# Mixing product tile by tile with two extra weight slots, the norm's factor moved into Exp and Gelu, and expert numbers found in two halves

## The reference, cut to what matters

```python
xn = rmsnorm_2(h, norm1_g)
q_a, k_a, v_a, q_b, k_b, v_b, gate_a, gate_b = split(xn @ w_in)
y_a = merge(moba_attention(...)) @ w_out_moba
y_b = merge(stick_breaking_attention(...)) @ w_out_sb
mixed = sigmoid(gate_a) * y_a + sigmoid(gate_b) * y_b
h = h + mixed @ w_mix_out
h = h + peer_ffn(rmsnorm_2(h, norm2_g), w_q, sub_keys, expert_u, expert_v)
return rmsnorm_2(h, final_norm_g)
```

```python
qh = (x @ w_q).reshape(8, 2, 128)
scores = einsum('hpc,hpnc->hpn', qh, sub_keys)            # 2 x 128 scores
s_top, i_top = top_k(scores, 16)                           # of each half
cand = s_top[0][:, None] + s_top[1][None, :]               # 256 sums
c_s, c_pos = top_k(cand, 16)                               # 16 experts of 16384
e = i_top[0][c_pos // 16] * 128 + i_top[1][c_pos % 16]
a = gelu(u[e] @ x); out += (softmax(c_s) * a) @ v[e]
```

## Time and profile before

| | |
|---|---|
| median of 3 runs | 1776.45 us (1774.53 to 1779.31) |
| profiled execution | 1774.82 us, span 1773.1 us |
| mean granted clock of TensorE | 0.981 of 2.4 GHz |
| busy: TensorE, VectorE, ScalarE, POOL | 1621.1, 1128.0, 849.2, 351.9 us |
| moved: gathers, other loads | 268.45 MB, 194.29 MB |

### The profile page before, as it was taken

How to read it: one execution, slowest core, us unless ns; L and a number is a source line. 1 busy time by engine, 2 the same in 40 slices (tenths; PEclk the granted TensorE clock), 3 DMA queues, 4 the chain that set the end, 5 groups by cost and what they waited for, 6 DMA issues and landing times.

```text
span 1773.1 us, 22582 instructions
## 1 busy us (share of the span) xinstructions
PE 1621.1 (91%) x8800; PEld 1222.6 (69%) x8800; DVE 1128.0 (64%) x1993; ACT 849.2 (48%) x1578; POOL 351.9 (20%) x368
## 2 busy tenths in 40 slices
PE   6999999999999999999989998899978788778786
PEld 5998998999898999899979997555522222222232
DVE  4747766555665776655555566778667667767744
ACT  4546635444455653544445644455444444444443
POOL 0100000000010000000040100555544444334440
PEclk9999999999999999999999999899999999999999
DMA  6544353555544346455544354999999999999996
GB/s 251 196 144 143 140 216 144 200 186 188 194 153 140 136 167 217 158 203 185 185 153 148 143 194 187 387 412 421 420 422 421 421 421 422 422 421 422 421 421 257
DMA packets 67066, 464.51 MB, mean 262 GB/s; under 512 B 7440, under 2 KB 9616, under 8 KB 11536
## 3 DMA queue, kind: packets, MB, share of 16 engines
q0 software_dynamic: 36864, 268.45, 36.5%
q1 hardware_dynamic: 29808, 194.29, 30.4%
q10 hardware_dynamic: 288, 0.33, 0.1%
HBM read 462.00 MB, written 1.05 MB: 261 GB/s over the span
## 4 chain that ended last, share of the span: by engine, by line
PE 67%; DMA 20%; DVE 5%; issue 4%; ACT 3%; POOL 0%; SPq 0%; POOLq 0%; ACTq 0%; DVEq 0%
PE acc L541 15%; PE acc L542 15%; PE acc L543 15%; DMA arena<-in_peer_uv,arena 8%; DMA row_w_lo<-in_peer_uv,arena 7%; PE acc L1621 4%; DMA row_w_hi<-in_peer_uv,arena 4%; PE acc L1624 4%; PE att L543 3%; PE att L542 3%; PE att L541 3%; DVE w_lo L537 1%; ACT w_hi L530 1%; PE att L839 1%; ACT gate_raw L1750 1%
## 5 line engine op out<-in xcount | busy, mean ns | idle before, releaser
L537 DVE TENSOR_TENSOR w_lo<-arena,w_hi 128x2048 fp32r<-128x2048 f32 x176 | 404.7, 2302 | 200.9 <-ACT w_hi L530 200.6
L530 ACT CAST w_hi<-arena 128x2048 fp32r<-128x2048 f32 x176 | 335.4, 1907 | 150.4 <-PE acc L543 139.0
L541 PE MATMUL acc<-xa_hi,w_hi 128*128 128x256 f32 x928 | 266.3, 287 | 0.0
L542 PE MATMUL acc<-xa_hi,w_lo 128*128 128x256 f32 x928 | 263.2, 284 | 0.0
L543 PE MATMUL acc<-xa_lo,w_hi 128*128 128x256 f32 x928 | 263.2, 284 | 0.0
L1742 ACT ACTIVATE arena<-arena 128x1 f32<-128x1 f32 x256 | 51.9, 203 | 313.8 <-DVE arena L2023 143.3
L2023 DVE SCALAR_TENSOR_TENSOR arena<-arena 128x1024 f32<-128x1024 f32 x114 | 139.4, 1223 | 84.7 <-DMA arena<-in_peer_uv,arena 84.6
L541 PEld LDWEIGHTS acc<-xa_hi,w_hi 128*128 128x128 f32 x928 | 178.5, 192 | 4.1 <-issue 3.1
L542 PEld LDWEIGHTS acc<-xa_hi,w_lo 128*128 128x128 f32 x928 | 178.5, 192 | 0.2
L543 PEld LDWEIGHTS acc<-xa_lo,w_hi 128*128 128x128 f32 x928 | 178.5, 192 | 0.0
L1621 PE MATMUL acc<-arena,gate_raw 128*128 128x512 f32 x228 | 129.5, 651 | 49.4 <-ACT gate_raw L1750 49.3
(11 more groups left out here) (295 smaller groups left out, 3352.4 us busy)
## 6 DMA issues: line engine op xcount, KB each, us to landing
arena<-in_units SPq DMA_DIRECT2D x176, 1024.0 KB, 4.8
arena<-in_bias SPq DMA_DIRECT2D x1, 2048.0 KB, 9.2
arena<-in_peer_uv,arena POOLq DMA_INDIRECT x114, 36.2
x_res<-in_x SPq DMA_DIRECT2D x2, 512.0 KB, 4.2
arena<-in_norm_mix_g SPq DMA_DIRECT2D x2, 512.0 KB, 6.6
arena<-in_norm_mlp_g SPq DMA_DIRECT2D x2, 512.0 KB, 6.5
arena<-in_norm_g SPq DMA_DIRECT2D x2, 512.0 KB, 5.7
arena<-in_final_norm_g SPq DMA_DIRECT2D x2, 512.0 KB, 5.7
```

What stands on the lines that cost most here:

```text
L530: nc.scalar.copy(w_hi[:, s, :], raw[HOME[g]]).then_inc(S["hi_ready"], 1)
L537: nc.vector.tensor_tensor(w_lo[:, s, :], raw[HOME[g]], w_hi[:, s, :].bitcast(F32), ALU.subtract).then_inc(S["lo_ready"], 1)
L541: nc.tensor.matmul(out_, lh, rh, start=first, stop=False)
L542: nc.tensor.matmul(out_, ll, rh, start=False, stop=False)
```

## The change

It has four parts.

1. The units of the mix come in the order 0, 2, 1, 3, and TensorE makes all four on tile 0 before it finishes tile 1. Mix 0 and pq 0 get weight slots of their own (`more_hi`, `more_lo`, laid over the biases, `mo` and `qk`); from yab 1 on the splits run three units ahead (`splits_at`). The loads of pq 5 and 6 wait for mix 0, since they lie where its parts are. The sub-keys are loaded ahead of unit ga2 0 and transposed after yab 0. Tile 1's queries of head 0 come after the whole mix.
2. The norm ahead of the experts no longer multiplies by one over the root: `hn` is x times the norm's weights, made half by half behind each add; the order of scores isn't changed by a positive factor for each token, and the factor is given as `scale` to Exp (of the score differences) and to Gelu. The squares (`peer_square`) come later, into memory of their own.
3. Head 0's first eight experts of tile 0 are looked up as soon as the eight largest sums are found, the next eight after; POOL waits for each eight. Tile 1's adds come behind head 0's whole routing on VectorE (`mix_second_tile`).
4. 18 places instead of 17, with other memory and other opening times: places 0 and 1 over mix 3's slot, 2 and 3 over `xa`, 4 and 5 over pq 0's slot, 6 and 7 over the raw slots of pq 2 and 3 (from items 6 and 8 on).

```diff
-PLACES = 17
-OPEN_FROM = [0] * 5 + [5, 6, 20, 30, 40, 50] + [72] * 6
+PLACES = 18
+OPEN_FROM = [0] * 4 + [4, 4, 6, 8, 20, 30, 40, 50] + [72] * 6
...
-    u += [("mix", i, "T") for i in range(4)] + [("pq", i, "F") for i in range(8)]
+    u += [("mix", i, "T") for i in (0, 2, 1, 3)] + [("pq", i, "F") for i in range(8)]
...
-SLOT = [g % RING for g in range(QUERY0 + 2)] + [(QUERY0 + h % 2) % RING for h in range(2, P_HEADS)]
+MIX0 = QUERY0 - 4
+SLOT = [g % RING for g in range(MIX0)] + [RING] + [(g - 1) % RING for g in range(MIX0 + 1, QUERY0)] + [RING + 1]
+SLOT += [SLOT[QUERY0 - 3 + (h + 1) % 2] for h in range(1, P_HEADS)]
...
-        rows_ring = slot_rows(q2) + [area("mo", 0, ROW), row_over("xa_hi", 0), row_over("xa_lo", 0)]
+        rows_ring = slot_rows(q3) + [row_over("xa_hi", 0), row_over("xa_lo", 0), area("mo", 0, ROW), area("qk", 0, ROW)]
...
+                if unit == ("ga2", 0, "F"):
+                    sp.wait_ge(S["hn_ready"], at("hn_ready", ("n1", TT - 1)))
+                    for h in range(HP):
+                        sp.dma_start(raw_keys[:, h, :], A["peer_sub_keys_2"][0, h // 2, h % 2]).then_inc(
+                            S["keys_loaded"], mark("keys_loaded", h, 16))
+                elif unit == ("mix", 0, "T"):
...
-            for h in (0, 1, 2, 5, 6, 7, 3, 4):
-                if h == 5:
-                    sp.wait_ge(S["pair_mx"], at("pair_mx", (PAIRS - 1, 1, 1)))
-                elif h == 7:
+            for h in (0, 1, 2, 7, 3, 5, 6, 4):
+                if h == 7:
                     sp.wait_ge(S["y_ready"], at("y_ready", 3))
+                elif h == 5:
+                    sp.wait_ge(S["unit_done"], at("unit_done", ("u", at_unit2["mix", 0])))
                 unit_dma(sp, at_unit2["pq", h])
...
+            if g == MIX0:
+                act.wait_ge(S["pair_mx"], at("pair_mx", (PAIRS - 1, 1, 1)))
+            elif g == QUERY0:
+                act.wait_ge(S["keys_ready"], at("keys_ready", 3))
+            elif USER[g] is not None and counts.scope == "second" and USER[g] >= DEPTH * NU:
+                act.wait_ge(S["unit_done"], at("unit_done", ("u", USER[g] - DEPTH * NU)))
...
+            return [] if u == 0 else [u + 2] if u < yab1 else [u + 2, u + 3] if u == yab1 else [u + 3]
...
+            def mix_first_tile():
+                mix_part(0, 0, range(4), True, False)
+                mix_part(2, 0, range(4), True, False)
+                mix_part(1, 0, range(4), False, True).then_inc(S["tile_done"], mark("tile_done", ("mix", 0)))
+                mix_part(3, 0, range(3), False, False)
+                half_pe(pe, 0, 0)
+                mix_part(3, 0, range(3, 4), False, True).then_inc(S["tile_done"], mark("tile_done", ("mix", 1)))
...
+                mix_part(3, 1, range(2), True, False)
                 pe.wait_ge(S["lo_ready"], QUERY0 + 1)
                 emptied2(pe, "mix", 0)
-                emptied2(pe, "mix", 1)
-                queries_of(0, 0, range(8))
+                queries_of(0, 0, range(4))
+                half_pe(pe, 0, 1)
+                emptied2(pe, "mix", 2)
                 queries_of(0, 1, range(4))
+                queries_of(0, 0, range(4, 8))
+                queries_of(0, 1, range(4, 6))
                 rank_half(0)
-                tile_pe(pe, "n2", 1)
-                queries_of(0, 1, range(4, 8))
-                queries_of(1, 0, range(2))
+                queries_of(0, 1, range(6, 8))
+                done(mix_part(3, 1, range(2, 4), False, False), 3)
                 rank_half(1)
-                queries_of(1, 0, range(2, 8))
+                done(mix_part(0, 1, range(4), True, False), 0)
+                done(mix_part(2, 1, range(4), False, True), 2)
+                done(mix_part(1, 1, range(4), False, True), 1)
+            def other_tile_queries():
+                half_pe(pe, 1, 1)
+                half_pe(pe, 1, 0)
+                queries_of(1, 0, range(8))
                 queries_of(1, 1, range(8))
...
-                nc.scalar.activation(w, w, ACT.Exp, accum_out=wsum[:, g:g + 1]).then_inc(
+                if g % P_HEADS == 0:
+                    act.wait_ge(S["rstd_ready"], at("rstd_ready", ("n2", g // P_HEADS)))
+                t = g // P_HEADS
+                nc.scalar.activation(w, w, ACT.Exp, scale=peer_rstd[:, t:t + 1], accum_out=wsum[:, g:g + 1]).then_inc(
...
-                nc.scalar.activation(d, d, ACT.Gelu).then_inc(S["gelu_ready"], 1)
+                t = n // SLOTS
+                nc.scalar.activation(d, d, ACT.Gelu, scale=peer_rstd[:, t:t + 1]).then_inc(S["gelu_ready"], 1)
...
-                if (name, i) == ("mix", 0):
+                if (name, i) == ("yab", 0):
                     keys_take()
-                elif (name, i) == ("mix", 3):
-                    norm_act(act, "n2", 0)
-                    split_hi(act, at_unit2["pq", 1])
-                    tile_act(act, xb_hi, "n2", 0)
-                    norm_act(act, "n2", 1)
+            split_hi(act, at_unit2["mix", 3])
+            split_hi(act, at_unit2["pq", 0])
+            half_act(act, 0, 0)
+            half_act(act, 0, 1)
             first_take(0)
             first_rank(0)
-            tile_act(act, xb_hi, "n2", 1)
             first_take(1)
             first_rank(1)
+            peer_square(0)
+            split_hi(act, at_unit2["pq", 1])
+            half_act(act, 1, 1)
+            half_act(act, 1, 0)
+            weight_exp(0)
+            peer_square(1)
+            split_hi(act, at_unit2["pq", 2])
             take("pq", 0)
-            split_hi(act, at_unit2["pq", 2])
...
+                dve.wait_ge(S["emptied_dve"], at("emptied_dve", ("mix", 2 * half + t)))
+                nc.vector.tensor_tensor(hn[:, t, 512 * half:512 * (half + 1)], piece, g_peer[:, 512 * half:512 * (half + 1)], ALU.mult).then_inc(
+                    S["hn_ready"], mark("hn_ready", ("n2", t, half)))
...
+                    if g == 0:
+                        experts(t, h, slice(0, 8), ("top8_at", (t, h, 2)))
                     top_next(t, h, sums)
+                elif g == 0:
+                    experts(t, h, slice(8, P_TOP), ("next8_at", (t, h, 2)))
...
+            def mix_first_tile():
+                split_lo(dve, at_unit2["mix", 3])
+                split_lo(dve, at_unit2["pq", 0])
+                dve.wait_ge(S["tile_done"], at("tile_done", ("mix", 0)))
+                dve.wait_ge(S["g_loaded"], at("g_loaded", "n2"))
+                mix_add(0, 0)
+                half_dve(dve, 0, 0)
                 dve.wait_ge(S["tile_done"], at("tile_done", ("mix", 1)))
                 mix_add(1, 0)
-                dve.wait_ge(S["g_loaded"], at("g_loaded", "n2"))
-                norm_dve(dve, "n2", 0, g_peer)
-                tile_dve(dve, xb_hi, xb_lo, "n2", 0, [0])
-                unit("mix", 3)
+                half_dve(dve, 0, 1)
+            def mix_second_tile():
+                unit("mix", 2)
                 mix_add(1, 1)
-                tile_dve(dve, xb_hi, xb_lo, "n2", 0, [1])
-                norm_dve(dve, "n2", 1, g_peer)
-                tile_dve(dve, xb_hi, xb_lo, "n2", 1)
+                unit("mix", 1)
+                mix_add(0, 1)
+                half_dve(dve, 1, 1)
+                half_dve(dve, 1, 0)
...
+                if n % P_TOP == 0 or n == 8:
                     g = n // P_TOP
...
-                elif 5 <= PLACE[n] < 11:
-                    pool.wait_ge(S["lo_ready"], QUERY0 + PLACE[n] - 5 + 2 + 1)
-                elif PLACE[n] >= 11:
+                elif PLACE[n] < 2:
+                    pool.wait_ge(S["unit_done"], at("unit_done", ("u", at_unit2["mix", 3])))
+                elif PLACE[n] < 4:
+                    pool.wait_ge(S["unit_done"], at("unit_done", ("u", at_unit2["mix", 1])))
+                elif PLACE[n] < 6:
+                    pool.wait_ge(S["unit_done"], at("unit_done", ("u", at_unit2["pq", 0])))
+                elif PLACE[n] < 12:
+                    pool.wait_ge(S["lo_ready"], QUERY0 + PLACE[n] - 6 + 2 + 1)
```

More of the change, by code:

```diff
@@ L1712, in keys_take, with peer_square @@
                         S["keys_ready"], mark("keys_ready", b))
+            def peer_square(t):
+                for half in range(2):
+                    act.wait_ge(S["emptied_dve"], at("emptied_dve", ("mix", 2 * half + t)))
+                nc.scalar.activation(square, x_res[:, t, :], ACT.Square, scale=D ** -0.5, accum_out=peer_ssq[:, t:t + 1]).then_inc(
+                    S["ssq_ready"], mark("ssq_ready", ("n2", t)))
             def first_take(i):
                 act.wait_ge(S["query_done"], at("query_done", (0, i)))
-                nc.scalar.copy(queries[:, i, 0:P], acc[i][:, i * SEQ:i * SEQ + P]).then_inc(S["query_in"], mark("query_in", i))
+                nc.scalar.copy(queries[:, i, 0:P], acc[2 * i][:, i * SEQ:i * SEQ + P]).then_inc(S["query_in"], mark("query_in", i))
             def first_rank(i):
                 act.wait_ge(S["rank_done"], at("rank_done", (0, 0, i)))
```

(16 more changed lines are left out.)

158 lines of the change are left out of this document (92 added, 66 removed).

## The result

The changed kernel takes 1784.30 us (median of 6 runs, 1783.35 to 1785.07) against 1776.46 us (median of 6 runs, 1774.53 to 1779.98) for the kernel before: a ratio of 1.0042, 95% interval 1.0033 to 1.0052. It is slower by 7.8 us, by more than the 0.3% that was named as the bound of what can be told. The forecast of 1779.5 was 4.8 us too low; rival 2, TensorE's clock, had 1784.4. Of the signs that the prediction named, two were missed, both on that side: row 0's product came at 1135.0 (named: 1127 to 1132), and the hole in the stream of gathers was 16.1 us (named: 7 to 12). The profiled execution took 1784.11 us, 9.3 more than that of before.

A forecast was written before the change was run, and what follows sets the result against it. The stream of gathers was taken to set the end, timed by first gather and row 0's product. Profiled 1774.82 + 1.9 net stream + 0.2 scales + 1.1 clock = 1778.0, median forecast 1779.5; own range 1775.5 to 1781.8, wider range 1771.0 to 1785.5.

The forecast's parts named there:

- rival 2: TensorE's waits cost in full, queries of tile 1 and head 1 at 1.2 GHz, late losses kept: 1784.4 us, chance 0.22.
- The two clocks: Stream of gathers: its timing hangs on the first gather (5.8 us earlier) and row 0's product (later, at 1128.1).
- rival 1: The first gather decides and the stream does not idle after gather 3: all 5.8 us count, 1770.6 us, chance 0.15.
- The yab stage: Stage before the mix: take of yab 3 moves from 1068.8 to 1072.9, and mix 2 waits 4.0 us.
- First gather: Tile 0's path to the first expert lookup: first gather issued at 1102.1, 5.8 us earlier.
- Tile 1: Tile 1's adds on VectorE follow head 0's routing: start 1105.3, transposes and rounding done 1110.3, queries end 1115.6.
- The clock: TensorE's waits ahead of mix 2 and tile 1's queries: half clock costs 1.1 of at most 4.1 us.
- The ring: Gather buffers: gathers 4 and 5 wait for pq 0's unit_done, gather 7 for row 0; DMA idles 8.7 us.
- Late losses: Later stream: today's losses of 0.7 and 1.0 us should go, thanks to more slack; 1.7 us taken as gain.
- Scales: Gelu on ScalarE with its scale read from memory: 0.09 us more a row, 0.2 us on the path.

The follow-up runs named there:

- one_lookup: Changed kernel with head 0's 16 expert numbers of tile 0 found in one go again, as before the change: 1782.07 us, 1.0031 of the kernel before.
- fill_tile1: Changed kernel with unread products only in TensorE's waits ahead of tile 1's transposes and queries, none ahead of mix 2: 1777.31 us, 1.0010 of the kernel before.
- fill_both: Changed kernel with unread products keeping TensorE busy ahead of mix 2, tile 1's transposes and tile 1's queries: 1778.21 us, 1.0014 of the kernel before.
- place7_at_7: Changed kernel with the ring's eighth place opened from item 7 on instead of 8: 1783.84 us, 1.0043 of the kernel before.
- rows_first: late_half with rows 0 to 3 used before head 1's queries instead of after them, and eighth place from item 12: 1781.78 us, 1.0031 of the kernel before.
- rows2_first: rows_first with only rows 0 and 1 ahead of head 1's queries, and the eighth place from item 10: 1782.16 us, 1.0034 of the kernel before.
- late_half: Changed kernel with the lookup of experts 8 to 15 and softmax differences moved behind tile 1's adds on VectorE: 1779.86 us, 1.0024 of the kernel before.
- rows8: rows_first with dot products 0 to 7 ahead of pq 3's split and coefficients 0 to 7 ahead of head 1's query copy: 1778.23 us, 1.0012 of before.

## Why the prediction was right or wrong

- **The two clocks** (first gather, row 0's product): right as a reading, and for the changed kernel the weighing of the two was right too. The early gather was worth nothing (one_lookup), so rival 1 falls.
- **The yab stage.** Predicted: take of yab 3 at 1072.9, a wait of 4.0 us ahead of mix 2. Measured: 1072.68 and 3.77. The half clock behind it cost TensorE 2.9 us (14 products of mix 2 0.43 us apart instead of 0.23), where the prediction had 0 to 1.7 for this wait, and VectorE 1.0 us ahead of tile 0's first add. By the medians of fill_tile1 and fill_both it has no weight at the end; by the traces it can have 1.4 us.
- **First gather.** Predicted 1102.1, with the second search at 1095.2 and 2.4 us for a lookup of eight. Measured 1102.12, 1095.46 and 2.27 (1099.44 to 1101.71). The sub-keys' loads, costed at nothing, held up nothing.
- **Tile 1.** Predicted: adds from 1105.3, parts ready at 1110.3. Measured 1105.30, and the last part ends at 1110.5.
- **The clock: the step that failed.** The mechanism stood in the prediction, as a term and as rival 2; the size was wrong. The prediction took 1.1 of at most 4.1 us. Measured, tile 1's queries took 10.3 us instead of 5.3 and head 1's 7.4 instead of 5.75, 6.6 us in all, of the 6.9 us by which row 0's product comes behind the 1128.1 of the forecast. The bound itself was too low: it was taken from what head 1's products lost before the change (2.4 us; there the clock was back some 5 us after work had begun again, 1109.32 to about 1114.4). In the changed kernel the clock came back 13.8 us after work had begun again, although the pauses ahead of it, 3.43, 0.67 and 1.40 us with four transposes after each of the first two, are all shorter than the 6.37 us of before. That a shorter pause costs less was an assumption, and the row that it leaned on (0.36 us of pause, clock kept) was too far away to carry it. The Trainium skill (TensorE: Matmul & The Clock Gate, section on why this matters for your kernels) has the engine back at half rate after an idle gap between bursts; the trace agrees, with 0.50 granted from 1110 to 1120.
- **The ring.** Predicted: gathers 4 to 6 wait for tile 1's queries, gather 7 for row 0, 8.7 us idle. By its own times it is 9.4: between 1117.4 and 1118.1 another 0.7 us lie idle. The order and the releasers are what the trace shows, and 9.4 with the clock's 6.6 is 16.0, measured 16.1. With the clock held (fill_both) gather 7 is issued at 1131.86, predicted 1132.1.
- **Late losses.** Predicted gone: from 1150 on the stream carries 418 to 426 GB/s, where the earlier trace rows had 392 and 378. Right. Rival 2 had kept them (1.7 us) and had 4.1 us for the clock; the clock cost 2.5 more and the losses were gone. Two errors nearly cancel, so it is in part luck that its 1784.4 meets the 1784.3.
- **Scales.** Gelu takes 293 ns instead of 203 (in the page's list, 256 times); on the path 0.2 us at most, which nothing here could tell from none.
- **The chances.** Slower by over 0.3% had 0.22 and is what came; within 0.3% had 0.63. The range, 1771.0 to 1785.5, holds the time only because it was drawn past rival 2; the forecast's own range ended at 1781.8.

The sum with the measured terms: gather 7's bytes at 1141.0 instead of 1130.7 is 10.3 us later, less 1.7 for the late losses, 8.6. The stretches behind 1750 show the stream's end: at 421 GB/s they hold 13.4 us of work against 4.6 before, so it ends 8.8 us later, and the last product comes 9.1 later. The last gather is issued only 7.7 us later (1731.69 against 1724.01), but that is no measure of the stream: with 18 places instead of 17 it waits for a row one earlier.

## What to carry to other kernels

When a change makes one engine wait at a place where it had only short pauses, cost all of the work behind the wait at the low clock, and only then ask for reasons why it should be less; whether it matters is settled in one run with idle products in the wait. A stream that starts earlier gains nothing if the buffers that it needs next are freed by a chain that starts later: count for each buffer in turn what frees it and when. And when a hole in the stream closes at one place and opens at another, look at the list of the engine behind it for the one instruction with work for the critical engine queued behind it; here it was first VectorE's split, then ScalarE's coefficient.

## What the runs showed of the hardware that was not expected

How long TensorE's clock stays low does not follow the length of the pause ahead. Before: a pause of 6.37 us, then 1.2 GHz for 5.1 us of products of 256 columns. Changed: pauses of 3.43, 0.67 and 1.40 us, then 1.2 GHz for 13.8 us, 10.3 us of it products of 128 columns one behind the other with no pause. Nor is it the same from one execution to the next: behind the same wait of 3.8 us ahead of mix 2 the clock stayed low for 6.8 us in five kernels (changed, one_lookup, place7_at_7, rows_first, rows2_first) and for 3.4 us in three (fill_tile1, late_half, rows8). Nor does the fall need a long pause. Before, it came at 1104.3, 1.3 us after the last product had ended. In late_half, with no pause above 1.40 us from 1103 on, the first 14 products of tile 1's queries still ran at 2.4 GHz, the clock fell at 1108.3 while the engine was at work (the spacing goes from 0.11 to 0.21 us), and came back at 1118.5:

```profile
1108.18 0.31 PE L563 MATMUL acc<-xb_hi,unit_qk 128*128 128x128 f32 x1
1108.29 0.41 PE L564 MATMUL acc<-xb_lo,unit_mo 128*128 128x128 f32 x1
```

In all four kernels with this order in which it fell ahead of tile 1's queries (changed, late_half, one_lookup, place7_at_7) it rose 2.0 to 3.7 us after head 1's wider products had begun, never during tile 1's. What decides that was not tried.

The mean time of a Gelu on one column goes from 203 to 293 ns when its scale is read from memory.
